# The order of a gate unit and a later tile's scores within each step of an attention stage

## The reference

```
proj = u @ w_in
q, k, v, us, g_att, g_ssm = split(proj)          # heads 8 x 64; the gates are 2 x 1024 wide
for window, dilation in ((128, 1), (512, 4), (2048, 16)):
    o, lse = dilated_window_attention(q, k, v, alibi_slopes, window, dilation)
o_att = sum(softmax(lse over the three) * o)
y_att = o_att @ w_proj_att
y_ssm = s5_branch(us) @ w_proj_ssm
merged = sigmoid(g_att + gb_att) * y_att + sigmoid(g_ssm + gb_ssm) * y_ssm
h = x + gate * (merged @ w_out)
```

## Time and profile before

| what | us |
|---|---|
| median of the runs | 2041.53 |
| the three runs | 2040.7, 2041.53, 2043.28 |
| profiled execution, its own time | 2039.93 |
| profiled execution, span of its trace | 2038.2 |
| attention stage in the trace, first scores to the last gate unit | about 231 to 548 |

### The profile page before, as it was taken

How to read it: one execution, slowest core, us unless ns; L and a number is a source line. 1 busy time by engine, 2 the same in 40 slices (tenths; PEclk the granted TensorE clock), 3 DMA queues, 4 the chain that set the end, 5 groups by cost and what they waited for, 6 DMA issues and landing times. The chain is left out here.

```text
span 2038.2 us, 25797 instructions
## 1 busy us (share of the span) xinstructions
PE 2010.5 (99%) x10043; PEld 1676.9 (82%) x10043; DVE 1086.4 (53%) x1397; ACT 647.1 (32%) x1068; POOL 1305.1 (64%) x757
## 2 busy tenths in 40 slices
PE   7999999999999999999999999999999999999998
PEld 3788988888888887788888888888888888888888
DVE  7981256555562485665632277731554555535554
ACT  3302232332331264534400035433434433321103
POOL 2538545665255539999944555976787888859750
PEclk9999999999999999999999999999999999999999
DMA  9545546444444204323475240334133322198432
GB/s 372 143 97 165 192 133 182 131 139 150 160 165 159 110 23 143 103 96 132 162 284 194 82 157 22 124 121 128 63 124 129 120 104 89 46 347 303 144 135 83
DMA packets 188360, 293.24 MB, mean 144 GB/s; under 512 B 12920, under 2 KB 136784, under 8 KB 188240
## 3 DMA queue, kind: packets, MB, share of 16 engines
q1 hardware_dynamic: 178256, 268.53, 38.9%
q10 hardware_dynamic: 9984, 23.07, 2.9%
HBM read 211.64 MB, written 79.94 MB: 143 GB/s over the span
## 5 line engine op out<-in xcount | busy, mean ns | idle before, releaser
L964 POOL TENSOR_SCALAR w_h<-raw 128x512 fp32r<-128x512 f32 (+2 forms) x108 | 237.4, 2198 | 334.1 <-issue 144.8
L1511 PE MATMUL ps<-tb,w_h 128*128 128x512 f32 x1344 | 416.7, 391 | 2.6 <-DVE quads L2798 1.9
L1049 POOL TENSOR_TENSOR w_l<-raw,w_h 128x512 fp32r<-128x512 f32 x210 | 308.9, 1480 | 96.9 <-ACT w_h L2068 96.9
L1511 PEld LDWEIGHTS ps<-tb,w_h 128*128 128x128 f32 x1344 | 251.3, 188 | 59.1 <-issue 3.9
L1511 PE MATMUL ps<-tb,w_l 128*128 128x512 f32 x672 | 261.5, 389 | 0.0
L966 POOL TENSOR_TENSOR w_l<-raw,w_h 128x512 fp32r<-128x512 f32 (+2 forms) x108 | 200.3, 1854 | 9.0
L2068 ACT ACTIVATE w_h<-raw 128x512 fp32r<-128x512 f32 x210 | 130.8, 627 | 235.3 <-PE ps L1511 150.3
L1511 PE MATMUL ps<-act_h,w_h 128*128 128x512 f32 x504 | 196.3, 390 | 0.6 <-ACT quads L2097 0.5
L1511 PE MATMUL ps<-act_h,w_l 128*128 128x512 f32 x504 | 196.1, 389 | 0.0
L1511 PE MATMUL ps<-act_l,w_h 128*128 128x512 f32 x504 | 196.1, 389 | 0.0
L1511 PEld LDWEIGHTS ps<-tb,w_l 128*128 128x128 f32 x672 | 126.1, 188 | 26.4
(11 more groups left out here) (414 smaller groups left out, 4610.2 us busy)
## 6 DMA issues: line engine op xcount, KB each, us to landing
raw<-in_w_in SPq DMA_DIRECT2D x44, 1024.0 KB, 5.2
raw<-in_w_up SPq DMA_DIRECT2D x16, 1024.0 KB, 5.2
f_scratch<-r SPq DMA_DIRECT2D x16, 1024.0 KB, 8.1
gates_scratch<-quads SPq DMA_DIRECT2D x24, 512.0 KB, 7.6
r<-gates_scratch SPq DMA_DIRECT2D x12, 1024.0 KB, 6.0
ada_lo<-in_w_ada SPq DMA_DIRECT2D x16, 512.0 KB, 3.6
ada_hi<-in_w_ada SPq DMA_DIRECT2D x16, 512.0 KB, 4.3
gates_scratch<-gate_st ACTq DMA_DIRECT2D x32, 256.0 KB, 2.0
```

What stands on the lines that cost most here:

```text
L964: nc.gpsimd.tensor_scalar(w_h[:, k, c, :], src[:, c, :], 1.0, None, ALU.mult).then_inc(s["w_high"], 1)
L1049: nc.gpsimd.tensor_tensor(w7_l[:, SLOTS[o]], x, w7_h[:, SLOTS[o]].bitcast(F32), ALU.subtract)\
L1511: last = nc.tensor.matmul(bank_of(n, bank), w[:, SLOTS[o], c, :], x(c), start=(first and c == 0 and p == 0), stop=(c == KD // 2 - 1 and p ...
```

## The change

In TensorE's step the gate part and the scores change places. No instruction is added or removed, and no other engine's program changes. The prelude ahead of the loop and the steps behind the loop's last scores stay as they are.

```
             for t in range(NT):
+                if t + 1 < NT - 2:
+                    gate_part(t + 1)
                 if t + 3 < NT:
                     scores(t + 3)
-                if t + 1 < NT - 2:
-                    gate_part(t + 1)
                 if t + 1 < NT:
                     transposes(t + 1)
```

## The result

The changed kernel takes **2047.91 us** in the median of 7 runs (2046.17 to 2048.68), the kernel before 2042.65 in 7 runs (2040.31 to 2044.6). The ratio is 1.0027, with a 95% interval of 1.0017 to 1.0037: 5.3 us slower, 3.5 to 7.6 by the interval. Of the 2.9 us by which it misses 2045.0, 1.1 belong to the kernel before, whose median was 2041.53 in three runs and is 2042.65 in seven; the change itself costs 1.8 more than the 3.5 that I had forecast.

A forecast was written before the change was run, and what follows sets the result against it. TensorE was taken to bound the kernel, without idle time in the steady attention stage. Gate waits 3.5 us, border 0 and later scores 0 gave 2041.53 + 3.5 = 2045.0 us, called the same; the 8-in-10 range was 2041.0 to 2048.0.

The forecast's parts named there:

- TensorE as the bound, a loss arrives at the end: Attention stage: TensorE never idles in the steady part, so a microsecond it loses there arrives at the end nearly whole.
- Where the wait appears: Even gate parts wait for ScalarE's gate read-out at 7 four-block and 7 three-block short tiles, not at one- or two-block ones.
- The price at a four-block place, 0.42: Gate part behind a four-block tile's values: read-out 0.34 late, 0.05 passing on, second product 0.34 later; 309.94 against 309.52.
- The weight load passes the wait: Rival at the gate part's wait: load goes ahead, 0.31 per four-block place, 2.2 in all, 2043.7 us; chance 0.08.
- The three-block places, 7 x 0.08: Gate part behind a three-block tile's values: read-out ends 299.81 against the place at 299.80, costing 0.08 at each of 7.
- The border, 0: Values followed by a wide product: the uncovered weight load's 0.08 moves from scores to gate part; bounds 4.9 gained, 1.8 lost.
- Later scores, VectorE 0: Short tiles' scores come 2.74 later, VectorE's minimum some 2.5; the delay ends in VectorE's idle time, price 0.
- a sign of being wrong: Attention stage in the trace after: longer by more than the waits it shows, or more than 14 waiting places.
- the border grows: Rival: gate parts behind values run at the pace of one behind transposes, 3.5 + 1.8 = 5.3, 2046.8 us; chance 0.22.
- my limit at 4.1: Whole kernel: a change below 0.2%, 4.1 us, can hardly be told from none and is called the same.
- "the same": Verdict on the whole kernel's time, a change within 4.1 us: chance 0.66, against slower 0.32 and faster 0.02.
- all the cases with a smaller loss than 3.5: Rivals: load passes the wait 2043.7 us, 0.08; border vanishes 2040.1, 0.06; change does nothing 2041.5, 0.06.

The follow-up runs named there:

- the waits taken away: The whole change, with ScalarE in even turns reading the gate sum ahead of its copy of the transposed tile: 2042.77 us, 1.0000 against the kernel before.
- the pieces first: The whole change, with VectorE in even turns doing the modulation pieces ahead of the short tile's minimum: 2048.25 us, 1.0023 against the kernel before.
- double read-out: The kernel before, with ScalarE reading each of the first 31 gate sums twice, first into spare memory: 2044.96 us, 1.0013 against the kernel before.

## Why the prediction was wrong, point by point

- **TensorE as the bound, a loss arrives at the end**: right. 4.66 in the stage, 4.47 at the end of the trace.
- **Where the wait appears**: right. The seven four-block places show 2.0 us of wait in the list; at the three-block ones it is too short for the list, and the step lengths show it. One- and two-block places show none.
- **The price at a four-block place, 0.42**: the lateness of 0.34 was right, and so was the sum, 0.418, but the sum by luck, since its other parts came out otherwise and cancelled. Passing on the release took 314.17 - (313.34 + 0.68) = 0.15 instead of 0.05, the second product followed after 0.31 instead of 0.34, and the scores gave 0.07 back.
- **The weight load passes the wait** (the rival by the rule of the Trainium skill, 0.31 per place): refuted by the rows. The second product follows the first by 0.31 at the four-block place and by 0.33 at the three-block place, not by the steady 0.23, and at three-block places the load stands at 304.21, together with its product and 0.05 behind the end of the read-out at 304.16, and not ahead of it.
- **The three-block places, 7 x 0.08**: a little small; they measure 0.10, 0.72 in all.
- **The border, 0**: the burden did change its owner as said (the first distance is 0.31 behind values in the gate part, and in the scores 317.20 - 316.98 = 0.22 now), but not evenly: the steps without a wait or a late product cost +0.54 in the change, and all steps +0.32 with the waits taken away. This lies between the bounds of -4.9 and +1.8, nearer to 0 than to either.
- **Later scores, VectorE 0**: here a step failed. The delayed minimum does not reach the half copies, as I said: 27 of the 30 stand against the values where they stood, and three come 0.7 to 0.8 later, behind the long pieces. Its largest delay against the values is 2.75, where I had estimated some 2.5. But I had followed only that path and left GpSimd out. TensorE also waits for VectorE's pieces of the modulation product, at line 1291, and three of these products came late, each behind a piece that ran beside a GpSimd instruction. Price 0.42. The minimum is not the cause as far as the runs go: at the three places it starts within 0.06 of where it did before.

The step that failed is thus the sum, by its two terms taken as 0: 0.54 for the border and 0.42 for VectorE, whose cause stays open. With 0.16 more at the three-block places and 0.07 ahead of the steps, the forecast 3.5 becomes 4.7. The waits at the 14 places measure 2.92 + 0.72 = 3.64, close to what I worked out. The stage is longer by 4.66, more than these waits, which I had named as a sign of being wrong. The rival "the border grows" gave the difference that came, 5.3, but not its cause: its term of 1.8 measured 0.54. And with my limit at 4.1, only 0.6 above the sum, and each of the two terms free to rise by as much, 0.66 for "the same" was too sure: all the cases with a smaller loss than 3.5 had 0.20 together.

What stays open: the medians differ by 5.3 and the traces by 4.5 to 4.7. The difference is inside the interval of 3.5 to 7.6, and no run here was made to split it.

## What to carry to other kernels

Work that seems to stand somewhere in the stream of the engine that is the bound may be the cover for another engine's hand-over. Before moving it, list each wait that would stand right behind what went ahead of it, and compare the release with the new place; here the lateness was paid in full at each place, and its price could be worked out from the rows of the kernel before to within 0.02 us per place. Where a loss is forecast near the limit of what counts, do not put small terms at 0: follow **every** reader of what another engine makes, not only the nearest one. And look for the release that could be made earlier instead: here one idle engine, doing its read-out ahead of its copy, takes nearly the whole loss away.

## What the runs showed of the hardware

- **Pieces of VectorE beside GpSimd.** The groups of VectorE, 236 to 540 us, hold one instruction on the same 128x256 operands in every kernel. Before, after, with the read-out first, and with the pieces first its mean is 511, 901, 1288 and 390 ns:

```profile
L2660 DVE TENSOR_SCALAR ada_part<-ada_lo,c_act 128x256 f32<-128x256 f32 x16 | 8.2, 511 | 0.0
```

```profile
L2660 DVE TENSOR_SCALAR ada_part<-ada_lo,c_act 128x256 f32<-128x256 f32 x15 | 13.5, 901 | 0.0
```

```profile
L2660 DVE TENSOR_SCALAR ada_part<-ada_lo,c_act 128x256 f32<-128x256 f32 x16 | 20.6, 1288 | 0.0
```

```profile
L2660 DVE TENSOR_SCALAR ada_part<-ada_lo,c_act 128x256 f32<-128x256 f32 x16 | 6.2, 390 | 0.0
```

Its length depends on where it falls against GpSimd's instructions, and a change of order on TensorE moves that. Where the mean was longest of these four, 1288, no product of line 1291 was late, so the mean alone tells nothing of the time. The Trainium skill, page "SBUF — State Buffer", section "SBUF: two separate sides", says that VectorE, in some of its instructions, and GpSimd take one pair of ports in turns, each for a whole instruction. The row of 2.49 above agrees: it ends 0.28 behind GpSimd's instruction (298.73 against 298.45). In all ten traces 28 pieces of line 2662 start inside an instruction of line 966; they take 2.48 to 2.56 us and end 0.28 to 0.29 behind it. Beside line 964 the rule does not show in this way: there the first of the two pieces of the kernel before lies wholly inside GpSimd's instruction (289.30 to 292.07) and takes the usual 0.48, as 162 of 219 pieces do in the ten traces that start inside one; the others take up to 1.22. Line 966 reads two tiles and line 964 one; that this is the reason was not tested.

- **Passing on a release** took 0.05 us at three-block places, where the gate product waits for the read-out alone, and 0.15 at four-block places, where it has a second wait, for the split weights. That the second wait makes the difference was not tested.
- **The clock dips near 100 us** in most profiles of this study, two kernels without any change of TensorE's order among them (the kernel before with ScalarE's early or double read-out), and not in that of the kernel before itself. The first score product stands between 230.72 and 234.19. The 61 runs of the kernel before that stand beside the experiments have a mean granted clock of 0.997 to 1.000, so executions of one kernel differ in this too, and a stage is to be compared with the same stage, and not a span with a span.
- **The steps repeat closely.** In the kernel before with either edit of ScalarE alone, every step up to the tail, but for the seven four-block ones with the double read-out, has its old length to within 0.001 us, and with the change the places of one class agree to 0.003 from the second head on. This is why differences of 0.02 us could be read here.
